# Mixers of a two-part transformer kernel: forget sums, query rotations, values and two norms in other places of the order

## What is computed

```python
z = rmsnorm_2(h, mix_norm[l]) @ w_in[l]
(c_q, c_kv, k_pe, z_u, z_v, hq, hf, hi, hg, rq, rk, rv, rg) = jnp.split(z, split_points, axis=-1)
y_a = mla_mixer(c_q, c_kv, k_pe, positions, ...)   # latent attention, queries and keys partly rotated
y_b = spatial_gating_mixer(z_u, z_v, ...)
y_c = hgrn2_mixer(hq, hf, hi, hg, lb_all[l], hg_norm[l])   # recurrence with a forget gate
y_d = retention_mixer(rq, rk, rv, rg, positions, ret_norm[l])
h = h + jnp.concatenate([y_a, y_b, y_c, y_d], axis=-1) @ w_out[l]
```

## Time and profile before

| | |
|---|---|
| Median of 3 runs | 3207.74 us (3207.02 to 3207.91) |
| Profiled execution | 3204.7 us |
| Its span | 3203.4 us, mean granted clock 0.990 |
| TensorE busy | 97% |
| GpSimd, VectorE, ScalarE busy | 69%, 46%, 22% |
| Mixers of layer 0 / layer 1 | 1366 to 1606 us / 2484 to 2722 us of the span |
| DMA | 273 MB, 85 GB/s |

### The profile page before, as it was taken

The page is one execution under the profiler, slowest core; times in us unless marked ns, Lnnn a source line. Parts: engine busy times, 40 slices in busy tenths (PEclk is TensorE's granted clock), DMA queues, the critical chain, the costliest instruction groups (busy, mean ns, idle before and its releaser), DMA issues.

```text
span 3203.4 us, 38552 instructions
## 1 busy us (share of the span) xinstructions
PE 3111.9 (97%) x14819; PEld 2515.2 (79%) x14819; DVE 1479.4 (46%) x2222; ACT 714.4 (22%) x1343; POOL 2207.5 (69%) x2524
## 2 busy tenths in 40 slices
PE   7999999999999999998999999999999998999998
PEld 5777777888888888887688888788888876888886
DVE  2347755677426631476643321533314876533214
ACT  2332222222111110233421110211102334211103
POOL 3546566999878887744378777777777443777775
PEclk8999999999999999999999999999999999999999
DMA  4212122333323333321123333333323211233332
GB/s 132 62 53 80 58 68 73 99 99 99 99 93 104 97 99 99 92 60 46 46 80 99 98 97 102 92 93 99 99 94 95 56 52 40 86 99 97 101 99 79
DMA packets 467568, 273.22 MB, mean 85 GB/s; under 512 B 20735, under 2 KB 463025, under 8 KB 467385
## 3 DMA queue, kind: packets, MB, share of 16 engines
q1 hardware_dynamic: 466328, 268.65, 28.4%
q10 hardware_dynamic: 1056, 2.12, 0.2%
HBM read 268.58 MB, written 2.12 MB: 85 GB/s over the span
## 4 chain that ended last, share of the span: by engine, by line
PE 91%; DVE 5%; POOL 1%; ACT 1%; issue 1%; SPq 0%; DMA 0%; DVEq 0%; POOLq 0%; ACTq 0%
PE bank L681 18%; PE bank L686 18%; PE bank L682 17%; PE bank L1112 6%; PE bank L1117 6%; PE bank L1111 6%; DVE arena L2090 2%; PE bank L975 2%; PE bank L715 1%; PE bank L781 1%; PE bank L1271 1%; PE bank L717 1%; PE bank L782 1%; PE bank L716 1%; POOL wl L646 1%; PE bank L846 1%
## 5 line engine op out<-in xcount | busy, mean ns | idle before, releaser
L646 POOL TENSOR_TENSOR wl<-raw,wh 128x256 fp32r<-128x256 f32 x2016 | 1656.5, 853 | 42.1
L641 POOL TENSOR_SCALAR wh<-raw 128x1024 fp32r<-128x1024 f32 x504 | 552.3, 1096 | 928.7 <-PE bank L686 369.8
L681 PE MATMUL bank<-xh,wh 128*128 128x512 f32 x1568 | 617.8, 394 | 0.1
L682 PE MATMUL bank<-xl,wh 128*128 128x512 f32 x1568 | 611.1, 390 | 0.0
L2090 DVE TENSOR_TENSOR arena<-arena 128x512 f32<-128x512 f32 (+3 forms) x478 | 412.3, 879 | 61.7 <-ACT arena L1826 10.4
L686 PE MATMUL bank<-xh,wl 128*128 128x512 f32 x1568 | 390.4, 389 | 0.6 <-POOL wl L646 0.6
L2090 DVE TENSOR_TENSOR arena<-bank,nrm 128x512 f32<-128x512 f32 x236 | 152.4, 685 | 513.0 <-PE bank L686 512.6
L681 PEld LDWEIGHTS bank<-xh,wh 128*128 128x128 f32 x1568 | 294.8, 188 | 71.3 <-issue 4.6
L686 PEld LDWEIGHTS bank<-xh,wl 128*128 128x128 f32 x1568 | 294.2, 188 | 62.1 <-POOL wl L646 1.0
L682 PEld LDWEIGHTS bank<-xl,wh 128*128 128x128 f32 x1568 | 294.8, 188 | 61.2 <-issue 1.2
L681 PE MATMUL bank<-arena_rounded,wh 128*128 128x512 f32 x816 | 318.8, 391 | 1.8 <-DVE arena L2090 1.8
(11 more groups left out here) (329 smaller groups left out, 4268.9 us busy)
## 6 DMA issues: line engine op xcount, KB each, us to landing
raw<-in_ffn_w_gate SPq DMA_DIRECT2D x176, 256.0 KB, 3.1
raw<-in_ffn_w_up SPq DMA_DIRECT2D x176, 256.0 KB, 3.1
raw<-in_ffn_w_down SPq DMA_DIRECT2D x176, 256.0 KB, 2.9
raw<-in_w_in SPq DMA_DIRECT2D x158, 256.0 KB, 3.1
raw<-in_w_up SPq DMA_DIRECT2D x88, 256.0 KB, 3.1
raw<-in_w_gate SPq DMA_DIRECT2D x64, 256.0 KB, 2.9
raw<-in_w_out SPq DMA_DIRECT2D x48, 256.0 KB, 3.0
raw<-in_w_down SPq DMA_DIRECT2D x44, 256.0 KB, 2.9
```

Source lines behind the costliest of these rows:

```text
L641: pool.tensor_scalar(wh[:, s, :], raw[:, s, :], 1.0, 0.0, ALU.mult, ALU.add).then_inc(split, 1)
L646: ins = pool.tensor_tensor(wl[:, s, c], raw[:, s, c], wh[:, s, c].bitcast(F32), ALU.subtract)
L681: pe.matmul(psum, cols(wh, i), xhi, start=(i == 0), stop=False)
L682: pe.matmul(psum, cols(wh, i), xlo, start=False, stop=False)
```

## The change

Six edits, all of them places in the order:

- `sums(2)` goes from unit 9 to unit 3, `sums(3)` from unit 11 to unit 4.
- The rotation of the first pair of queries is read a head at a time on VectorE: head 0 in unit 25, head 1 in unit 26. Before, both stood in unit 25.
- In the stream the rotation of the second pair stands before the latent values, no longer behind them.
- The recurrence's first norm goes from attention unit 1 to 3, its second from unit 5 to 4 (there behind the retention step of the unit).
- On TensorE retention's second `centred` goes from `between(11)` to `behind_values(10)`, and its second `mean_square` from `between(12)` to `behind_values(11)`.
- ScalarE's second `root` goes from unit 12 to 11. VectorE's `rstd` stays in unit 12.

```diff
--- before.py
+++ after.py
@@ -1239,7 +1239,7 @@
                 grains_tm(("hi", l), xk), rotations(("rot", 2, l), NH, 1, ("ckv", l)), grains_fm(("hq", 1, l), xk),
                 grains_fm(("rq", l), xk), grains_tm(("rv", l), xk), grains_fm(("rk", l), xk),
                 latent_queries(0), latent_queries(1), rotations(("rot", 0, l), 0, 2, ("uq", 0, l)), latent_keys(),
-                latent_values(), rotations(("rot", 1, l), 2, 2, ("uq", 1, l)), grains_fm(("zu", l), xk, 1),
+                rotations(("rot", 1, l), 2, 2, ("uq", 1, l)), latent_values(), grains_fm(("zu", l), xk, 1),
                 grains_tm(("zv", l), xk, 1), grains_fm(("rg", l), xk, 1), grains_fm(("hg", l), xk, 1),
                 spatial_mix())
             stop, due = [None], [0]
@@ -1415,10 +1415,6 @@
                 if u == 0:
                     pe.wait_ge(*T.at("evac", "rot", 1, l))
                     ret_swaps(0)
-                if u == 11:
-                    centred(1)
-                if u == 12:
-                    mean_square("r", 1, bank[3], gnr[1])
                 if u not in new_tile and u in grains:
                     fill(1)
                 if u == 1:
@@ -1446,6 +1442,10 @@
 
             def behind_values(u):
                 fill(grains.get(u, 0) - (u not in new_tile and u in grains))
+                if u == 10:
+                    centred(1)
+                if u == 11:
+                    mean_square("r", 1, bank[3], gnr[1])
 
             for key in ("uk", l), ("rot", 0, l):
                 pe.wait_ge(*T.at("evac", *key))
@@ -1994,8 +1994,8 @@
                 if u in (7, 11):
                     act.wait_ge(*A.at("centred", u // 11, l))
                     group_square("r", u // 11, gnr[1], bank[2][:, :])
-                if u in (8, 12):
-                    root(bank[3][:, :], "gms", "r", u // 12, l)
+                if u in (8, 11):
+                    root(bank[3][:, :], "gms", "r", u // 11, l)
                 if u == 8:
                     act.wait_ge(*A.at("sgvar", l))
                     act.activation(sgst[:, :, 3], sgst[:, :, 1], ACT.Ln, bias=eps[:, 0:1]).then_inc(*A.up())
@@ -2633,19 +2633,18 @@
                 v.copy_predicated(scT[:, hh % 2, :].rearrange("p (i t) -> p i t", i=TT), m,
                                   SC[n % 2][:, :].rearrange("p (i t) -> p i t", i=TT)).then_inc(*V.up("lvl_used", n, l))
 
-            def rotated(n):
-                for j in range(3):
-                    if done_at["rot", j, l] == n:
-                        s = evac_start(("rot", j, l))
-                        for i in range(1 if j == 2 else 2):
-                            x0 = kpe if j == 2 else qh[2 * j + i][64:96, :]
-                            t0 = qtmp[64:96, :]
-                            last()
-                            tt(t0, bank[2 * s + i][64:96, :], rope[64:96, 3, :], ALU.mult)
-                            tt(x0, x0, rope[64:96, 2, :], ALU.mult)
-                            last()
-                            tt(x0, x0, t0, ALU.add)
-                        V.same("evac", "rot", j, l)
+            def rotated(j, first, n):
+                s = evac_start(("rot", j, l))
+                for i in range(first, first + n):
+                    x0 = kpe if j == 2 else qh[2 * j + i][64:96, :]
+                    t0 = qtmp[64:96, :]
+                    last()
+                    tt(t0, bank[2 * s + i][64:96, :], rope[64:96, 3, :], ALU.mult)
+                    tt(x0, x0, rope[64:96, 2, :], ALU.mult)
+                    last()
+                    tt(x0, x0, t0, ALU.add)
+                if j == 2 or first + n == 2:
+                    V.same("evac", "rot", j, l)
 
             def recurrence_normed(c, y, t):
                 rstd_last(("h", c, l), None, y, t)
@@ -2678,9 +2677,9 @@
                     tt(kpe, bank[2 * s + 1][64:96, :], hrstd[64:96, :], ALU.mult, "evac", "ckv", l)
                 if n == 2:
                     sums(1)
-                if n == 9:
+                if n == 3:
                     sums(2)
-                if n == 11:
+                if n == 4:
                     sums(3)
                 if lv == 3 and hh < NH - 1:
                     tail(hh + 1)
@@ -2710,9 +2709,11 @@
                 if done_at["rk", l] == n - 1:
                     rows_out(("rk", l), rk, HD ** -0.5)
                 if n == 8:
-                    rotated(done_at["rot", 2, l])
+                    rotated(2, 0, 1)
                 if n - 1 == done_at["rot", 0, l]:
-                    rotated(n - 1)
+                    rotated(0, 0, 1)
+                if n - 2 == done_at["rot", 0, l]:
+                    rotated(0, 1, 1)
                 if (hh, lv) == (3, 0):
                     rstd_first(PT[:, :], ("h", 0, l))
                 if n == UNITS - 1:
@@ -2770,7 +2771,7 @@
                     rstd_first(OB[:, :], ("h", 1, l), gnt[:, 1, :], qtmp)
                 if u in (0, 2):
                     ret_rotated(u)
-                if u == 1:
+                if u == 3:
                     recurrence_normed(0, nrm[:, 1, :], nrm[:, 2, :])
                 if u in (9, 12):
                     rstd(bank[3][:, :], ("r", u // 12, l))
@@ -2807,7 +2808,7 @@
                            rq[:, c, :].rearrange("p (i t) -> p i t", i=TT),
                            R("query", c)[:, None, :].to_broadcast([P, TT, P]), ALU.mult,
                            *(("rqd", l) if c else ()))
-                if u == 5:
+                if u == 4:
                     recurrence_normed(1, gnt[:, 1, :], qtmp)
                 if u in (6, 7):
                     v.wait_ge(*V.at("zv", l))
@@ -2846,7 +2847,7 @@
                 src = (cq, zu, hgate, rgate)[i // 2][:, i % 2, :]
                 rest(f"lout{l}", i, src, *lout_operand(i))
 
-            attention(f"ml{l}", between, lambda: rotated(done_at["rot", 1, l]))
+            attention(f"ml{l}", between, lambda: rotated(1, 0, 2))
             spatial_out()
             for i in (2, 3):
                 lout_rest(i)
```

## The result

The changed kernel takes **3216.33 us** (median of 9 runs, 3214.48 to 3219.78), the kernel before 3207.74 us (9 runs, 3206.83 to 3208.99). The ratio is 1.0029, with a 95% interval of 1.0018 to 1.0039: slower, by some 9 us. The profiled execution of the changed kernel has a span of 3217.6 us against 3203.4. So a difference read between these two traces is not the difference of the medians to the last microsecond.

What follows compares the result with a forecast made beforehand. TensorE, busy 97% of the span, was taken as the bound. Terms -0.2 + 0 - 2.9 + 9.0 + 1.2 = +7.1 us took the profiled 3204.7 to 3211.8; with 3.0 for the median, 3214.8 us, range 3207.0 to 3219.5.

Steps and rivals of the forecast that it cites:

- Rotations: Before level 26: one TensorE wait of 3.4 us becomes two of 1.3 and 2.1, scores start unchanged; 0.
- Second norm: Attention unit 4: norm of 4.93 us delays unit 5's value products by 2.8 us plus 1.7 clock per layer; +9.0 us.
- Retention's norm: Centring product waits 0.75 us for ScalarE's copy; the 4.85 us wait comes no sooner; 0.6 per layer, +1.2 us.
- Rival (b): Not slower: norm at unit 4 runs near 2.93 us, stall 0.8 us without clock loss; 3207.4 us, chance 0.14.
- (c): Faster: short norm at unit 4, no clock loss at unit 26 or layer 1's new wait, retention free; 3201.1 us, chance 0.08.
- The swap by itself gives nothing: At zu, values last only moves the bank-pair wait from layer 0 to layer 1; net 0.
- -3.65 us ... +3.65 us: At zu: layer 0 sheds 1.95 us idle and 1.7 of clock, layer 1 takes on the same.
- Keeping the wait at 1.24: At zv, moving the first norm leaves layer 0's wait at 1.24 us; layer 1's 2.41 falls to about that.
- A sign of being wrong: Level waits of units 15 and 16 shrinking by more than 0.3 us would show the forecast wrong.
- The other sign: Value products of attention unit 5 not waiting would show the forecast wrong.
- Rival (a): Clock keeps 2.4 GHz over three new stalls (2.8 twice, 1.95 in layer 1); +2.0, 3209.7 us, chance 0.23.
- Rival (d): The moves do nothing, as orders on engines with slack change no end; excluded for two places, no chance given.

Runs made afterwards that it cites:

- the trial in layer 0 alone: Kernel before with the latent values put behind the second pair's rotation in layer 0 only, layer 1 keeping its old order: 3207.64 us, ratio 0.9999.

## Why the prediction was right, and where two of its terms were wrong

The forecast was 3214.8 us with a range of 3207.0 to 3219.5, and slower only just the likelier side (0.47, against 0.45 for no change); 3216.33 was measured. The parts alone add up to the whole: 0.01 + 0.06 + 0.20 - 0.27 + 0.23 + 0.02 = +0.25%, against +0.29% (0.18 to 0.39). Against this, by the prediction's steps:

| Part | forecast, us | alone, us (95%) |
|---|---|---|
| Forget sums | -0.2 | +0.3 (-2.6 to 3.2) |
| Rotations by heads | 0 | +1.9 (-1.3 to 4.8) |
| Values last (the swap) | 0 | +6.4 (3.8 to 9.3) |
| First norm | -2.9 | -8.7 (-12.2 to -5.5) |
| Second norm | +9.0 | +7.4 (4.8 to 10.3) |
| Retention's norm | +1.2 | +0.6 (-2.2 to 3.5) |

**Second norm: right in mechanism and size.** The wait was forecast at 2.8 and is 2.60; the norm at 4.93 and is 4.81. The clock's share was taken as 1.7 per layer: alone it is 1.6 and 1.4, in the changed kernel 3.1 and 2.9. Rival (b), a norm near its quiet 2.93 us, falls, and (c), which rests on it, with it. The Trainium skill (SBUF — State Buffer, Who interferes with whom) calls the port pair an exclusive lock; the 7.5 us that I had worked out from it for the norm don't bear out against 4.81 measured, so the four operations didn't each wait for a whole GpSimd instruction.

**Rotations: right.** One wait of 3.38 became 1.34 and 1.90 (1.3 and 2.1 forecast). Alone the part measures +1.9, with nothing inside its interval.

**"The swap by itself gives nothing": wrong, by 6 us.** The step "-3.65 us ... +3.65 us" took the price of the wait in layer 0 for layer 1, and counted only the wait that moves. It is 3.06 there (2.78 in the changed kernel), since GpSimd's next piece starts later and lands beside VectorE's rotations. And the step left out what stands behind unit 26's wait once the values are gone: 3.4 us more lost by the clock in layer 0, and 1.7 in layer 1 than in the kernel before. With both: layer 0 -1.95 - 1.7 + 3.4 = -0.2, as the trial in layer 0 alone measured (0), layer 1 +3.06 + 1.6 + 1.7 = +6.4. Together +6.2 against 6.4. The longer wait in layer 1 is sure, since three traces with the new order there have 2.8 to 3.1; the terms of the clock are less so. Most traces with the old order lost nothing behind the 1.95 in layer 0 and already 2.7 to 3.0 behind unit 26 in layer 1, and against those the same sum gives +1.5 and some +5.

**"Keeping the wait at 1.24": wrong.** With the norm gone VectorE took the score behind it 2.8 us sooner (the row maximum at 1513.64, where it was at 1516.43), read zu as soon as its last product had ended, and the wait is 0 alone and in the changed kernel. And the 1.24 of layer 0 came from one execution: three of the five traces with the order and the norm as before in layer 0 wait 2.4 us there. The clock at zu was read from the same execution: of the eight traces with the 1.95 us wait two lost 1.7 us behind it and six nothing.

These two misses nearly cancel (+6.4 and -5.8 beside the forecast), so that the sum came out right partly by luck.

**Retention's norm:** the wait at L1408 is 0.70 as forecast (0.75). The long wait shrank to 4.27 in most places where it was to stay 4.85, and so the term is nearer to nothing than +1.2, though its interval holds both.

**A sign of being wrong that came.** I had written that the level waits of units 15 and 16 must not shrink by more than 0.3 us. In layer 1 the wait of unit 15 fell from 1.51 to 1.14 us. The forget sums are not what did it, since the trace with the sums alone keeps 1.50; every trace with the rotations by heads has 1.13 to 1.15, and why is not shown. The other sign, value products of unit 5 that do not wait, did not come.

**Rival (a), the clock holding,** falls in all three places of the changed kernel's trace: the windows at 1.2 GHz stand behind 2.60, 2.60 and 2.78 us of waiting. Rival (d), that the moves do nothing, falls by the time.

## What to carry to other kernels

When two pieces of work change places, price three things: the wait that moves, what other engines start later because a buffer is freed later, and what TensorE runs directly behind the next long wait. Here the same 3.4 us wait cost 1.6 us of clock in layer 0 with the values next and 5.0 with the rotation next; whether it is the size of the products that counts was not tried. And an operation on VectorE that begins close to a split on GpSimd has two durations (0.75 and 1.52 us here, by which of the two began first), so read it in more than one trace before either goes into a sum.

## What the runs showed that was not expected

The loss of clock behind a wait isn't a constant. Behind 1.95 us at zu the kernel before lost 1.7 us, and the kernel with the first norm in unit 3 lost nothing behind the same 1.95 us; so did five others. Behind 2.60 us at unit 5 it was 1.4 to 1.6 us in five places and 2.8 to 3.1 in three, and those three are the layers whose values are made last. So the order and the second norm may not be independent: the new order stands with a dearer wait at unit 5. No run asks why. The windows of that first-norm kernel around the harmless wait:

```profile
1498.00:1500.00 2.00, 1.29 (x6) 1.00 0.00 0
1500.00:1502.00 2.00, 2.00 (x10) 1.00 0.00 0
```

There is also a loss in a place where TensorE doesn't wait at all. In the changed kernel 10 us with TensorE busy throughout are granted 0.84. The kernel before was granted 1.00 there; the traces of all twelve experiments show such a dip between 2070 and 2090 us, the kernels that are faster than before too. So it is more likely that the profiled execution of the kernel before is the exception than that the change makes the dip. The window in the changed kernel:

```profile
2080.00:2090.00 10.00, 10.00 (x37) 7.73 (x36) 0.60 (x1) 2.00 (x4) 6.49 (x9) 0.84 0.18 52
```

What brings it about stays open; at 1.6 us it is inside the spread of the runs.
